# Rows of v before the small tables, state outputs on the Pool queue, and turned probabilities in four PSUM banks

## The chip, the cores and the metric

The kernel runs on one core of a Trainium2 chip. The core has TensorE (PE; PEld is its weight load), VectorE (DVE), ScalarE (ACT), GpSimd (POOL) and the synchronisation engine SyncE (SP). Transfers are issued from SP, ScalarE and Pool and carried out by 16 DMA engines that all three share. The metric is the device time of one launch in microseconds (us); lower is better. All data are float32.

## The reference

One inference step of a hybrid decoder layer, for a prompt of 2048 tokens and for 8 sample sequences of 4 new tokens each, which have 8192 past tokens in a paged cache:

```python
h = rmsnorm(x, norm_g)
z = jnp.einsum('btd,de->bte', h, w_in)
q_a, k_att, v_a, f_a, g_a, sh_b, g_b, u_c, g_c, u_d, g_d = split_cols(z)
logf = jax.nn.log_sigmoid((f_a + fox_bf).astype(jnp.float32))
o_a = attend(qh, kh, vh, logf)          # A: attention with forget gates
o_b, wkv1, shift1 = rwkv7_mix(sh_b, ...)  # B: RWKV-7, a matrix state
o_c, pool1 = pool_mixer(u_c, ...)       # C: causal pooling
o_d, conv1 = conv_module(u_d, ...)      # D: convolution, width 31
mixed = jnp.concatenate([o_a * silu(g_a), o_b * silu(g_b), o_c * silu(g_c), o_d * silu(g_d)], axis=-1)
x = x + jnp.einsum('bte,ed->btd', mixed, w_out)
return x, kh, vh, logf, wkv1, shift1, pool1, conv1
```

Two pieces matter here. The recurrence of B, run for four steps on the samples:

```python
s_kk = jnp.einsum('bhvk,bhk->bhv', s, kk_t)
s = s * w_t[:, :, None, :] - s_kk[..., None] * (kk_t * a_t)[:, :, None, :] + v_t[..., None] * k_t[:, :, None, :]
o = jnp.einsum('bhvk,bhk->bhv', s, r_t)
```

And the attention of the samples over the cache, whose scores take the running sum of log-forget values, and whose result is `softmax(scores) @ v_all`. Keys, values, log-forget values and states of the new tokens are outputs too.

## The kernel before

Each engine runs a program of its own, written out by hand; semaphores tie them together, and the order of the calls in each engine's function is the order of its work. Nothing is scheduled by a planner. Most data live in one large tile, `big`, whose areas are reused from stage to stage. The stages, in order of time:

*Projection.* TensorE multiplies h by 25 column groups of w_in (`chunk`, matmuls at L795), ScalarE copies each result out of PSUM (L1379) and stores it to the DRAM tensor `zT`. Convolution, pooling and the inputs of B run beside it on VectorE.

*Sample steps (about 740 to 840 us).* In the last column groups TensorE puts `sample_step(0)` to `sample_step(4)` (matmuls L906 and L914), with `value_rows` (L881) between them. Step i needs the state after step i-1, which VectorE makes in four operations (L1858 to L1862) from `v_row[i]`, and VectorE first multiplies all four `v_row` tiles (L1851). A `v_row` is one row of v for each of 8 sequences, written by ScalarE to the DRAM tensor `zsD` and read back by SP at L495, repeated over 64 partitions for each of two halves. Before these multiplies VectorE computes the index tables `pidx` and `lidx` (L1832 to L1838), for which it waits until six small loads, the last of them `aux`, have landed:

```python
dve.wait_ge(rows_in, 16 * 6)
```

Pool waits for these indices and then issues 64 gathers of log-forget rows (L757, tile `scores_`), and later 64 gathers of cached values, four of which may be under way.

*Prompt attention (about 914 to 1260 us).* TensorE goes through 32 items (16 query blocks, 2 head pairs): `scores`, `turn` (L988), `values` (L1001). From item 6 on, `early_keys` adds a step of the samples' scores (L1014), for which SP must have loaded 16 pages of keys (`key_pages`, L547). SP's loop over the items issues the page loads for the next step, which wait for the step before (`sc_mm`), stores an item's output and loads a gate. At item 11 it issues seven outputs (L557 to L564). VectorE's `forget_sums` (L1959) scans the gathered log-forget values, first after item 3.

*B over the prompt (about 1260 to 1540 us)*, with the other 16 steps of keys between its matmuls.

*Turned probabilities (about 1540 to 1590 us).* ScalarE takes exponentials of `scores_` in 8 blocks of 1024 columns. TensorE turns each block with 8 transposes into two PSUM banks (`turn_probs`), and ScalarE copies the two banks back (`probs_turned`, L1613). Blocks 0 and 1 are turned between two groups of the sums that normalise B's output (L1314), the others after them. ScalarE runs squares, the copies of blocks 0 and 1, then logarithms and exponentials (L1410), then the other copies.

*Output.* `value_tile` (L1051) multiplies turned probabilities by gathered values, 10 tiles first and 54 between the matmuls of the output projection (L1341).

Of the kernel before, what the change touches and what calls it, by code (L numbers as in the profile page):

```python
# [11 lines left out]
P = 128  # L12
D_MODEL, SEQ, DEC_BATCH, DEC_SEQ = 1024, 2048, 8, 4
SMP = DEC_BATCH * DEC_SEQ
T_ALL = SEQ + SMP
# [71 lines left out]
def build(nc, I, O):  # L87
    ctx = ExitStack()
    with ctx:
# [370 lines left out]
        def _(sp):  # L460
# [25 lines left out]
            sp.wait_ge(rw_stored, 128)  # L486
            sp.dma_start(wvf, I['w_vf']).then_inc(pars_in, 16)
# [4 lines left out]
            sp.wait_ge(v_spread, 16 * DEC_SEQ)  # L492
            sp.dma_start(s_wkv[0], I['state_T']).then_inc(s_in, 16)
            for i in range(DEC_SEQ):
                sp.dma_start(v_row[i], zsD[i].unsqueeze(1).to_broadcast([2, 64, 1024])).then_inc(x_in[i], 16)  # L495
# [53 lines left out]
            for j in range(len(ITEMS) - 2):  # L549
# [5 lines left out]
                if j == 11:  # L555
                    for t in range(2):
                        sp.dma_start(O['kT'][t], zT[KA + t]).then_inc(st_stored, 16)  # L557
                    sp.wait_ge(vf_evac, TT + 1)
                    sp.dma_start(O['v_prompt'][0, 0].rearrange("(n p) h d -> p n (h d)", p=P), vtok[:, 0:TT, 0:256]).then_inc(st_stored, 16)
                    sp.dma_start(O['v_sample'].rearrange("b l t h d -> (b l t) (h d)"), vtok[0:SMP, TT, 0:256]).then_inc(st_stored, 16)  # L560
                    sp.wait_ge(nl_ready, 2)
                    sp.dma_start(O['logf_prompt'][0, 0].rearrange("(n p) h -> p n h", p=P), lo[:, 0:TT, :]).then_inc(st_stored, 16)
                    sp.dma_start(O['logf_sample'].rearrange("b l t h -> (b l t) h"), lo[0:SMP, TT, :]).then_inc(st_stored, 16)
                    sp.dma_start(O['shiftE'], zT[R0:R0 + 7, :, SEQ - 1:T_ALL]).then_inc(st_stored, 16)  # L564
# [90 lines left out]
        def _(pool):  # L655
# [98 lines left out]
            pool.wait_ge(idx_ready, 1)  # L754

# [5 lines left out]
            for t in range(N_PAGES):  # L761
                x = 1 + (N_PAGES - 1 - t) * PAGE
                gather(scores_[:, x:x + PAGE], cf, lidx[:, t:t + 1], lf_in)
            pool.wait_ge(sc_mm, KSTEPS)
# [7 lines left out]
        def _(pe):  # L772
# [494 lines left out]
            def turn_probs(blk):  # L1267
                pe.wait_ge(D['p'], D0['p'] + blk + 1)
                if blk == 0:
                    pe.wait_ge(D['neg'], D0['neg'] + 1)  # L1270
                else:
                    pe.wait_ge(D['pT'], D0['pT'] + 2 * blk)
                rows = scores_[:, blk * 1024:(blk + 1) * 1024].rearrange("p (x j) -> p j x", j=TJ)
                for j in range(TJ):
                    last = transpose(psum[:, 6 + j // 4, (j % 4) * P:(j % 4 + 1) * P], rows[:, TJ - 1 - j, :])
# [1007 lines left out]
```

## Time and profile before

| | us |
|---|---|
| median of three timed runs | 1932.46 |
| lowest and highest | 1923.53 and 1933.47 |
| profiled execution, its own time | 1928.07 |
| its span, first to last instruction | 1926.3 |

| engine | busy us | share of the span |
|---|---|---|
| PE | 1773.4 | 92% |
| PEld | 1094.4 | 57% |
| DVE | 776.4 | 40% |
| ACT | 477.7 | 25% |
| POOL | 174.9 | 9% |

The profile is that of one execution. A busy time says how long an engine had instructions under way, and tells nothing of which engine the others wait for. For that one reads the chain of waits and the timeline of each engine: a timeline row gives start, duration, engine, line, what is written and read, the count of merged instructions and, in brackets, how long the engine had been idle and what ended that. Positions below are us from the start of the span. The names of SP's, ScalarE's and Pool's queues end in q.

### The profile page before, as it was taken

The numbers are of one execution on the slowest core, as the hardware profiler recorded it, in microseconds if no ns is written. First come the engines' busy times: TensorE is split into PE (matmuls) and PEld (weight loads), VectorE is DVE, ScalarE is ACT, GpSimd is POOL, SyncE is SP. The second block draws the span as 40 slices with busy tenths as digits, with TensorE's granted clock in tenths as the row PEclk, the third lists the DMA queues.
The fourth block names the chain that finished last, engine by engine and source line by source line (L and its number), as shares of the span: only waits on it lengthen the run. The fifth ranks groups of instructions, "written<-read, shape, count | busy, mean of one in ns | idle before, by whom it ended". The sixth has DMA issues, their size and how long they took to land.

```text
span 1926.3 us, 35542 instructions
## 1 busy us (share of the span) xinstructions
PE 1773.4 (92%) x15076; PEld 1094.4 (57%) x15076; DVE 776.4 (40%) x1640; ACT 477.7 (25%) x855; POOL 174.9 (9%) x220
## 2 busy tenths in 40 slices
PE   6999999999999999299697999998989878999997
PEld 3555555555554555286464677788878743444442
DVE  3450699742221541311553554435545551112112
ACT  4301100010327231002343454422222270000000
POOL 1000000011000003720000000000000002111210
PEclk9999999999999999699798999999999978999998
DMA  6223320376312345231565324467655267788782
GB/s 228 78 84 106 121 88 34 135 191 164 118 67 89 132 166 190 85 122 27 169 197 134 98 86 141 145 208 227 187 153 155 91 260 290 275 298 272 273 290 72
DMA packets 154512, 300.77 MB, mean 156 GB/s; under 512 B 20285, under 2 KB 124589, under 8 KB 136238
## 3 DMA queue, kind: packets, MB, share of 16 engines
q1 hardware_dynamic: 131746, 154.72, 25.8%
q0 software_dynamic: 18240, 115.82, 17.6%
q10 hardware_dynamic: 4368, 27.96, 3.6%
q8 instruction: 119, 1.95, 0.4%
q14 instruction: 39, 0.32, 0.0%
HBM read 236.73 MB, written 63.96 MB: 156 GB/s over the span
## 4 chain that ended last, share of the span: by engine, by line
PE 71%; DVE 13%; DMA 6%; ACT 4%; issue 3%; SPq 2%; another core or an unknown queue 1%; POOL 0%; ACTq 0%; DVEq 0%
PE psum L795 22%; PE psum L1051 13%; PE psum L1341 13%; DVE big L1733 8%; PE psum L988 6%; PE psum L1014 3%; PE psum L881 3%; PE psum L1001 3%; PE psum L975 2%; DMA big<-zsD 2%; ACT big L1410 2%; PE psum L775 2%; PE psum L827 1%; DMA rkv<-big 1%; DMA big<-zT 1%
## 5 line engine op out<-in xcount | busy, mean ns | idle before, releaser
L795 PE MATMUL psum<-big,wbuf 128*128 128x416 f32 x1920 | 675.8, 513 | 5.6 <-DVE big L1663 3.4
L795 PEld LDWEIGHTS psum<-big,wbuf 128*128 128x128 f32 x1920 | 364.9, 190 | 311.9 <-issue 310.2
L1051 PE MATMUL psum<-big 64*64 64x64 f32 (+3 forms) x5792 | 218.6, 263 | 25.3 <-issue 12.1
L1051 PEld LDWEIGHTS psum<-big 64*64 64x64 f32 (+2 forms) x5792 | 165.1, 132 | 87.8 <-issue 53.7
L1379 ACT ACTIVATE zst<-psum 128x416 f32<-128x416 f32 x125 | 64.0, 517 | 539.1 <-PE psum L795 539.0
L1341 PE MATMUL psum<-big 128*128 128x512 f32 (+1 forms) x408 | 186.5, 607 | 1.1 <-issue 1.1
L757 POOL DMA_INDIRECT big<-in_cache_v,pidx x64 | 60.6, 947 | 986.5 <-PE psum L1014 684.6
L1733 DVE SCALAR_TENSOR_TENSOR big<-big,pars 128x2048 f32<-128x2048 f32 x120 | 148.2, 1298 | 1.1
L1341 PEld LDWEIGHTS psum<-big 128*128 128x128 f32 (+1 forms) x408 | 73.5, 187 | 97.6 <-issue 97.6
L2175 DVE TENSOR_TENSOR zst<-zst,psum 128x1024 f32<-128x1024 f32 (+1 forms) x17 | 20.7, 1220 | 229.6 <-PE psum L1341 229.6
L1641 ACT ACTIVATE big<-zst 128x1024 f32<-128x1024 f32 (+1 forms) x17 | 18.0, 1057 | 301.1 <-DVE zst L2175 301.1
L988 PE MATMUL psum<-big,zst 128*128 128x128 f32 x544 | 72.8, 286 | 10.8 <-DVE big L1937 10.4
L1529 ACT COPY wbuf<-psum 128x512 f32<-128x512 f32 (+3 forms) x80 | 41.5, 519 | 165.5 <-PE psum L988 165.5
L975 PE MATMUL psum<-big 64*128 64x512 f32 (+3 forms) x320 | 74.3, 574 | 5.9 <-DVE big L1911 5.2
L988 PE MATMUL psum<-big 128*128 128x128 f32 x544 | 73.1, 287 | 5.9 <-DVE big L1937 5.4
L1001 PE MATMUL psum<-wbuf,big 128*64 128x128 f32 x544 | 77.8, 283 | 0.0
L1001 PE MATMUL psum<-big 128*64 128x128 f32 x544 | 77.8, 283 | 0.0
L988 PEld LDWEIGHTS psum<-big,zst 128*128 128x128 f32 x544 | 65.2, 194 | 20.3 <-DVE big L1937 11.4
L988 PEld LDWEIGHTS psum<-big 128*128 128x128 f32 x544 | 65.5, 195 | 15.4 <-DVE big L1937 7.6
L1001 PEld LDWEIGHTS psum<-wbuf,big 128*64 128x64 f32 x544 | 58.1, 138 | 26.7 <-issue 18.6
L1014 PE MATMUL psum<-big,lora 128*32 128x256 f32 x864 | 55.6, 399 | 18.7 <-DMA big<-in_k_pages 14.7
L757 POOL DMA_INDIRECT big<-in_logf_rows,lidx x64 | 65.3, 1020 | 34.9 <-issue 19.2
(240 smaller groups left out, 1839.4 us busy)
## 6 DMA issues: line engine op xcount, KB each, us to landing
big<-in_k_pages SPq DMA_DIRECT2D x432, 128.0 KB, 2.3
zT<-zst ACTq DMA_DIRECT2D x25, 1040.0 KB, 6.7
wbuf<-in_w_slots SPq DMA_DIRECT2D x24, 512.0 KB, 4.7
big<-zT POOLq DMA_DIRECT2D x11, 1024.0 KB, 5.6
zst<-in_k_pages SPq DMA_DIRECT2D x80, 128.0 KB, 2.5
rwS<-big POOLq DMA_DIRECT2D x8, 1024.0 KB, 4.2
big<-rwS SPq DMA_DIRECT2D x8, 1024.0 KB, 5.8
zst<-in_x_prompt SPq DMA_DIRECT2D x16, 512.0 KB, 8.5
```

The source lines that it names most:

```text
L757: g.indirect_dma_start(out=dst, out_offset=None, in_=cache, in_offset=bass.IndirectOffsetOnAxis(ap=idx, axis=0)).then_inc(s, 16)
L795: last = nc.tensor.matmul(psum[:, m % CHUNKS, 0:CW], w[:, k, :], hT[:, k, c * CW:(c + 1) * CW], start=(k == 0), stop=(k == KT - 1))
L881: last = nc.tensor.matmul(psum[0:r, n % CHUNKS, 0:VF], hT[:, k, n * P:n * P + r], wvf[:, k, :], start=(k == 0), stop=(k == KT - 1))
L975: last = nc.tensor.matmul(psum[:, 2 * (b % 2) + h, 0:w], kq[hs, 1, pr, i * P:(i + 1) * P], kq[hs, 0, pr, c * 512:c * 512 + w], start=True, ...
L988: last = nc.tensor.matmul(psum[:, 4 + h, k * P:(k + 1) * P], rows_[j % 2][h][:, x:x + P], diag[:, j % 2, h, :], start=True, stop=True)
L1001: last = nc.tensor.matmul(psum[h * 64:h * 64 + 64, 6 + j % 2, 0:P], vtok[:, k, (2 * pr + h) * 64:(2 * pr + h + 1) * 64], probsT[h][:, k * ...
L1014: last = nc.tensor.matmul(psum[32 * ct:32 * ct + 32, bank, 0:256].rearrange("p (i c) -> p i c", i=2), qbd[:, pr, b * 32:(b + 1) * 32], pag ...
L1051: return nc.tensor.matmul(out, l, r, start=start, stop=stop, skip_group_check=True)
L1341: last = nc.tensor.matmul(psum[0:n, 2 * u + o, :], l, wo[e][:, o * 512:(o + 1) * 512], start=(k == 0), stop=(k == 7))
L1379: nc.scalar.activation(zst[:, u, c * CW:(c + 1) * CW], psum[:, m % CHUNKS, 0:CW], f, scale=0.125 if n in (QA, QA + 1) else 1.0).then_inc(z ...
L1529: nc.scalar.copy(probsT[h][:, c * 512:c * 512 + width(j, c)], psum[:, 4 + h, 0:width(j, c)]).then_inc(pT_ready, 1)
L1733: last = v.scalar_tensor_tensor(out, in_, w, out, ALU.mult, ALU.add)
```

## The change

Four edits, all in the order of transfers, in waits and in bank numbers; the computation is the same.

1. SP issues the loads of `s_wkv[0]` and of the four `v_row` tiles before those of `wvf`, the masks, `bf_b` and `aux`.
2. Pool waits for the four `v_row` loads before its first gather.
3. The seven outputs of item 11 move from SP's loop to Pool, behind the log-forget gathers and a wait for 12 finished items.
4. `turn_probs` and `probs_turned` use banks 6 and 7 for even blocks and 4 and 5 for odd ones, and a turn waits for the copies of the block two before it.

```diff
             sp.wait_ge(rw_stored, 128)
+            sp.wait_ge(v_spread, 16 * DEC_SEQ)
+            sp.dma_start(s_wkv[0], I['state_T']).then_inc(s_in, 16)
+            for i in range(DEC_SEQ):
+                sp.dma_start(v_row[i], zsD[i].unsqueeze(1).to_broadcast([2, 64, 1024])).then_inc(x_in[i], 16)
             sp.dma_start(wvf, I['w_vf']).then_inc(pars_in, 16)
             sp.dma_start(dmask, I['diag_mask']).then_inc(rows_in, 16)
             sp.dma_start(rw_masks, I['rw_masks']).then_inc(rows_in, 16)
             sp.dma_start(bf_b, I['fox_bf'].to_broadcast([P, 4])).then_inc(rows_in, 16)
             sp.dma_start(aux[:, :], I['aux']).then_inc(rows_in, 16)
-            sp.wait_ge(v_spread, 16 * DEC_SEQ)
-            sp.dma_start(s_wkv[0], I['state_T']).then_inc(s_in, 16)
-            for i in range(DEC_SEQ):
-                sp.dma_start(v_row[i], zsD[i].unsqueeze(1).to_broadcast([2, 64, 1024])).then_inc(x_in[i], 16)
...
                 gate_store(j)
-                if j == 11:
-                    for t in range(2):
-                        sp.dma_start(O['kT'][t], zT[KA + t]).then_inc(st_stored, 16)
...
             pool.wait_ge(idx_ready, 1)
+            for i in range(DEC_SEQ):
+                pool.wait_ge(x_in[i], X_SEEN[i] + 16)
...
                 gather(scores_[:, x:x + PAGE], cf, lidx[:, t:t + 1], lf_in)
+            pool.wait_ge(o_read, 12)
+            for t in range(2):
+                pool.dma_start(O['kT'][t], zT[KA + t]).then_inc(st_stored, 16)
+            pool.wait_ge(vf_evac, TT + 1)
...
             pool.wait_ge(sc_mm, KSTEPS)
...
-                else:
-                    pe.wait_ge(D['pT'], D0['pT'] + 2 * blk)
+                elif blk >= 2:
+                    pe.wait_ge(D['pT'], D0['pT'] + 2 * (blk - 1))
...
-                    last = transpose(psum[:, 6 + j // 4, (j % 4) * P:(j % 4 + 1) * P], rows[:, TJ - 1 - j, :])
+                    last = transpose(psum[:, 6 - 2 * (blk % 2) + j // 4, (j % 4) * P:(j % 4 + 1) * P], rows[:, TJ - 1 - j, :])
...
-                    nc.scalar.copy(scores_[:, x:x + 512], psum[:, 6 + hf, :]).then_inc(D['pT'], 1)
+                    nc.scalar.copy(scores_[:, x:x + 512], psum[:, 6 - 2 * (blk % 2) + hf, :]).then_inc(D['pT'], 1)
```

SP's order of issue behind the last column weights, before (-) and with the change (+); `zsD x4` are the four rows of v:

```order
 L467 DMA wbuf<-in_w_slots 128x1024 x18
-L487 DMA big<-in_w_vf 128x2080
-L488 DMA big<-in_diag_mask 128x128
-L489 DMA big<-in_rw_masks 128x256
-L490 DMA big<-in_fox_bf 128x4
-L491 DMA big<-in_aux 128x128
-L493 DMA big<-in_state_T 128x1024
-L495 DMA big<-zsD 128x1x1024 x4
+L488 DMA big<-in_state_T 128x1024
+L490 DMA big<-zsD 128x1x1024 x4
+L491 DMA big<-in_w_vf 128x2080
+L492 DMA big<-in_diag_mask 128x128
+L493 DMA big<-in_rw_masks 128x256
+L494 DMA big<-in_fox_bf 128x4
+L495 DMA big<-in_aux 128x128
 L499 DMA qT_s<-zT 128x32
```

The rows of v moved ahead of five other loads, of which `aux` is the last.

Pool's order of issue behind the last stores of B's inputs, with the change (lines of the changed kernel; in_logf_rows are the log-forget gathers, in_cache_v those of values):

```order
83 L749 DMA big<-in_logf_rows,lidx 128x128 [waits x_in1,x_in2,x_in0,x_in3,idx_ready,rw_stored]
84 L749 DMA big<-in_logf_rows,lidx 128x128 x63
85 L758 DMA out_kT<-zT 32x8320 [waits o_read]
86 L758 DMA out_kT<-zT 32x8320
87 L760 DMA out_v_prompt<-big 128x16x256 [waits vf_evac]
88 L761 DMA out_v_sample<-big 32x256
89 L763 DMA out_logf_prompt<-big 128x16x4 [waits nl_ready]
90 L764 DMA out_logf_sample<-big 32x4
91 L765 DMA out_shiftE<-zT 896x33
92 L749 DMA big<-in_cache_v,pidx 128x2048 [waits sc_mm]
```

Before, Pool's gathers of values followed its log-forget gathers directly, and these waited for `idx_ready` and `rw_stored` alone; the seven outputs stood on SP between an item's gate load and the next page loads:

```order
187 L511 DMA pars<-zT 128x128 [waits mixa_stored0]
188 L557 DMA out_kT<-zT 32x8320 x2
189 L559 DMA out_v_prompt<-big 128x16x256 [waits vf_evac]
190 L560 DMA out_v_sample<-big 32x256
191 L562 DMA out_logf_prompt<-big 128x16x4 [waits nl_ready]
192 L563 DMA out_logf_sample<-big 32x4
193 L564 DMA out_shiftE<-zT 896x33
194 L542 TENSOR_LOAD pwo [waits sc_mm]
196 L547 DMA big<-in_k_pages 128x256
```

With the change L542 follows L511 directly. On TensorE no instruction moved; only the waits of `turn_probs` and its banks differ.

## Rows read from the trace of the kernel before

**Rows 1.** The page, part 4: the chain that ended last, by engine.

```profile
PE 71%; DVE 13%; DMA 6%; ACT 4%; issue 3%; SPq 2%; another core or an unknown queue 1%; POOL 0%; ACTq 0%; DVEq 0%
```

**Rows 2.** TensorE's timeline: start, duration (us), engine, line, what, count, idle before.

```profile
805.75 3.57 PE L906 MATMUL psum<-big,smp 64*64 64x64 f32 x64 [38.50 <-DVE big L1862]
```

**Rows 3.** VectorE's timeline, 748 to 941.

```profile
748.28 0.19 DVE L1832 CAST pidf<-pidx 128x64 f32<-128x64 int32 x1 [18.83 <-DMA big<-in_aux]
...
749.29 0.20 DVE L1838 CAST pidx<-pidf 128x64 int32<-128x64 f32 x1
...
760.84 1.23 DVE L1851 TENSOR_TENSOR big<-big,smp 128x1024 f32<-128x1024 f32 x1 [11.35 <-DMA big<-zsD]
...
799.55 1.23 DVE L1851 TENSOR_TENSOR big<-big,smp 128x1024 f32<-128x1024 f32 x1 [10.81 <-DMA big<-zsD]
800.70 1.22 DVE L1858 TENSOR_TENSOR big<-big,smp 128x1024 f32<-128x1024 f32 x1
...
940.39 2.29 DVE L1959 TENSOR_TENSOR_SCAN big<-big 128x1024 f32<-128x1024 f32 x1
```

**Rows 4.** DMA queues, 749 to 752: packets, MB, share of 16 engines.

```profile
q1 hardware_dynamic: 38, 0.16, 12.8%
```

**Rows 5.** DMA queues, 749 to 799: q0 is Pool's, q1 SP's.

```profile
q0 software_dynamic: 1148, 2.35, 14.7%
q1 hardware_dynamic: 1052, 2.13, 11.3%
```

**Rows 6.** SP's timeline.

```profile
770.99 13.07 SPq L499 DMA_DIRECT2D qT_s<-zT  x1
```

**Rows 7.** The loads of qT_s, from the issue's end to landing.

```profile
DMA to landing us min/median/max: 4.2/9.9/15.5
```

**Rows 8.** SP's timeline, 999 to 1017.

```profile
999.21 1.23 SPq L557 DMA_DIRECT2D out_kT<-zT  x2
...
1001.11 7.43 SPq L560 DMA_DIRECT2D out_v_sample<-big  x1
...
1016.57 8.93 SPq L547 DMA_DIRECT2D big<-in_k_pages  x16
```

**Rows 9.** TensorE's timeline, 998 to 1033.

```profile
998.45 1.93 PE L1014 MATMUL psum<-big,lora 128*32 128x256 f32 x32 [0.73 <-issue]
...
1029.67 3.64 PE L1014 MATMUL psum<-big,lora 128*32 128x256 f32 x32 [14.32 <-DMA big<-in_k_pages]
```

**Rows 10.** Stretches: length, busy PE, PEld, DVE, ACT, POOL; granted clock, DMA share, GB/s.

```profile
999.00:1016.00 17.00, 16.35 (x160) 12.09 (x151) 8.88 (x42) 9.80 (x19) 0.00 (x0) 1.00 0.87 262
...
1020.00:1030.00 10.00, 0.33 (x4) 0.20 (x8) 0.00 (x0) 0.00 (x0) 0.00 (x0) 0.50 0.87 232
...
1572.00:1590.00 18.00, 10.56 (x51) 8.46 (x50) 17.50 (x33) 6.54 (x13) 0.00 (x0) 0.64 0.27 96
```

**Rows 11.** Line L1613 (copies of turned blocks), who waited for it: us, times.

```profile
  PE psum L775: 11.8, 7
```

**Rows 12.** TensorE's timeline, 1555 to 1596.

```profile
1555.85 1.35 PE L775 MATMUL psum<-ident,big 128*128 128x128 f32 x8 [4.34 <-ACT big L1613]
...
1572.46 1.05 PE L775 MATMUL psum<-ident,big 128*128 128x128 f32 x8
...
1583.55 1.94 PE L775 MATMUL psum<-ident,big 128*128 128x128 f32 x8 [1.25 <-ACT big L1613]
...
1590.60 5.38 PE L1051 MATMUL psum<-big 128*32 128x256 f32 x64
```

**Rows 13.** ScalarE's timeline, 1557 to 1590.

```profile
1557.23 1.07 ACT L1613 COPY big<-psum 128x512 f32<-128x512 f32 x2 [1.53 <-PE psum L775]
...
1588.72 1.07 ACT L1613 COPY big<-psum 128x512 f32<-128x512 f32 x2 [2.12 <-PE psum L775]
```

**Rows 14.** Pool's timeline: the first and the last of 64 gathers.

```profile
750.36 1.03 POOL L757 DMA_INDIRECT big<-in_logf_rows,lidx  x1 [15.73 <-DVE pidx L1838]
...
832.87 1.99 POOL L757 DMA_INDIRECT big<-in_logf_rows,lidx  x1 [0.30 <-issue]
```

More of the change, by code:

```diff
@@ L554, in _ @@
                 gate_store(j)
-                if j == 11:
-                    for t in range(2):
-                        sp.dma_start(O['kT'][t], zT[KA + t]).then_inc(st_stored, 16)
[L558 to L564, printed above, removed]
             sp.wait_ge(st_stored, 16 * 7)
@@ L763, in _ @@
                 gather(scores_[:, x:x + PAGE], cf, lidx[:, t:t + 1], lf_in)
+            pool.wait_ge(o_read, 12)
+            for t in range(2):
+                pool.dma_start(O['kT'][t], zT[KA + t]).then_inc(st_stored, 16)
+            pool.wait_ge(vf_evac, TT + 1)
+            pool.dma_start(O['v_prompt'][0, 0].rearrange("(n p) h d -> p n (h d)", p=P), vtok[:, 0:TT, 0:256]).then_inc(st_stored, 16)
+            pool.dma_start(O['v_sample'].rearrange("b l t h d -> (b l t) (h d)"), vtok[0:SMP, TT, 0:256]).then_inc(st_stored, 16)
+            pool.wait_ge(nl_ready, 2)
+            pool.dma_start(O['logf_prompt'][0, 0].rearrange("(n p) h -> p n h", p=P), lo[:, 0:TT, :]).then_inc(st_stored, 16)
+            pool.dma_start(O['logf_sample'].rearrange("b l t h -> (b l t) h"), lo[0:SMP, TT, :]).then_inc(st_stored, 16)
+            pool.dma_start(O['shiftE'], zT[R0:R0 + 7, :, SEQ - 1:T_ALL]).then_inc(st_stored, 16)
             pool.wait_ge(sc_mm, KSTEPS)
```

## The prediction

> **What bounds the kernel now.** I read the page's chain of waits first: TensorE carries 71% of it, so time is won only where TensorE stands idle [rows 1]. Then I looked on TensorE's timeline for idle stretches beside the edited lines. There are three, one for each part of the change.
>
> *Place A, the sample steps.* TensorE idles 38.50 us before the second recurrence step at 805.75 [rows 2]. VectorE explains it: it multiplies four rows of v, the first at 760.84 after its load, the last at 799.55, having waited 10.81 us for it, and the chain L1858 to L1862 starts at 800.70 [rows 3]. From there to TensorE's restart are 5.05 us. So the loads of v decide, one row every (799.55 - 760.84) / 3 = 12.9 us for 512 KB.
>
> Why so slow? In 749 to 752 they are the only traffic: 0.16 MB in 3 us, 52 GB/s, with 12.8% of 16 engines busy, which is 2.05 engines [rows 4]. Two engines are full and fourteen empty. With the gathers of log-forget rows beside them (14.7% of 16 engines) they hold 11.3% over 50 us [rows 5]. The small load of qT_s, whose issue ended at 770.99 + 13.07 = 784.06, landed up to 15.5 us later, at 799.56, the same moment as the last row [rows 6, 7]. A transfer that is spread over all engines therefore waits on the two busy ones for all rows issued ahead of it. That is the fact that part one turns on.
>
> *Place B, the state outputs.* SP issues seven output transfers from 999.21 on, and the issue at L560 alone holds it 7.43 us. Only then do the 16 loads of key pages go out, from 1016.57 [rows 8]. TensorE waits 14.32 us for them, from 1015.35 to 1029.67, and its first group then takes 3.64 us against 1.93 for the same 32 matmuls at 998.45 [rows 9]: the granted clock was 0.50 in 1020 to 1030 and 1.00 before [rows 10].
>
> *Place C, the turned probabilities.* ScalarE's copies (L1613) held TensorE up 7 times, 11.8 us in total [rows 11]. Block 1 waits 4.34 us, until 1555.85; the blocks from 1572.46 on go one at a time, each turn waiting 1.25 us for the copy of the one before and taking 1.94 us, and the value matmuls start at 1590.60 [rows 12]. ScalarE in turn waits for each turn [rows 13].
>
> **The change, part by part.**
>
> *A.* The four rows and state_T move ahead of w_vf, the two masks, fox_bf and aux. About 1.3 MB leave the queue ahead of them: 81 KB for each engine, at 26 GB/s per engine (half of 52) 3.1 us, and some 4.5 us with ScalarE's store of zT that shares the engines; I take 4.5. The rows themselves, alone on two engines, need 2.1 MB / 52 GB/s = 40.4 us, and 2.5 us more for the zT store that falls between them, 43 us instead of the 50.4 they took (799 minus a start at 748.5, one 12 us row before the first landing). So the last row lands 12 us earlier, near 787.5.
>
> But VectorE's order is not changed. It first waits for all six small tables (L1832), aux among them, before any multiply of v. Today aux is in at 748.28 [rows 3] and this wait is covered by the rows. Now aux sits behind all four rows on the two full engines, with w_vf and the masks between (again 1.3 MB, 3.1 us, and about 0.5 us to land): near 791. Behind it come the index arithmetic, 748.28 to 749.49 (1.2 us), four multiplies at 1.15 to 1.23 instead of one (4.9 us in all), and the 5.05 us chain: TensorE restarts near 802.2, not 805.75. **A gains 3.5 us.** Bounds: 0 if w_vf and the tables go out late, and 12 if aux does not queue behind the rows (787.5 + 1.2 + 5.05 = 793.8).
>
> The gathers get a wait for all four rows, but they need the indices that VectorE writes after aux, so they start near 792 in any case, 42 us later. Behind them on the Pool queue now stand the seven outputs. The 64 gathers are issued in 832.87 + 1.99 - 750.36 = 84.5 us [rows 14], so they end near 877; the first scan that needs them is at 940.39 [rows 3]. Cover of 60 us; the cost is nothing.
>
> *B.* The seven outputs go to Pool, which is idle there, and SP is free at 999.2. It must still wait for the key step before (it ends at 1000.4), so the page loads go out from about 1001.5 (1.2 us after, as now). The outputs start at the same time, since Pool waits for the same twelve finished items. What lies between is engine time: the outputs filled 0.87 of all engines for 17 us (14.8 us), the pages 0.87 of them for 10 us (8.7 us) [rows 10]. If pages wait for all outputs they land near 999.2 + 14.8 + 8.7 = 1022.7: gain 7. If they go first they land before TensorE asks at 1015.35: gain 14.3. With equal shares the pages need twice 8.7 us from 1001.5, 1018.9: TensorE waits 3.6 us, gain 10.7. I take equal shares, because the nearest rows with two queues on one engine, the rows of v beside the gathers, show both advancing [rows 5]. The matmuls at half clock give back 3.64 - 1.93 = 1.7 us more. **B gains 12.4 us**, bounds 7 and 16.
>
> Here two rules of the Trainium skill bear. The page DMA: Bandwidth & Descriptors (Queues, rings and completion order) says that an engine takes turns between queues packet by packet; kT's packets would be long and the pages' short, so by it the pages would lose most turns until kT is through, and B would fall towards its lower bound. The page SBUF — State Buffer (SBUF: two separate sides) says that transfers issued on Pool wait for their descriptors while VectorE runs certain copies; by it the outputs would trail, the pages would win, and B would come to its upper bound. Rows 5 decide between neither.
>
> *C.* Even blocks keep banks 6 and 7, odd ones get 4 and 5, so a turn waits for the copy two blocks back. Block 1 is turned at once at 1555.85 - 4.34 = 1551.5, and ScalarE's copy of it no longer waits 1.53 us [rows 13]. The logarithms behind it start 1.5 us earlier, and TensorE's group sums, which wait for the first of them, end near 1570.9, not 1572.46. From there ScalarE's copies set the pace: 1.1 us for the first turn, six blocks at 1.1 us (1.07 for two copies and the handover), and the 0.8 us that lie between the last copy (1588.72 + 1.07) and 1590.60: 1579.4. Gain 11.2, and the first value tile, done at half clock today, should be 0.5 us quicker. **C gains 11.7 us.** If the clock falls as it does today (0.64 in 1572 to 1590, [rows 10]), turns at 1.94 us pace it: 1570.9 + 1.1 + 6 x 1.94 + 0.8 = 1584.4, gain 6.2; the upper bound is 13. Banks 4 and 5 are free until the value tiles, and VectorE's gated output, ready at 1591, is wanted only after ten value tiles, so nothing takes the place of this wait. Behind it, the value gathers hang on the tiles and move along.
>
> **Sum.** 3.5 + 12.4 + 11.7 = 27.6 us. Against the profiled execution's 1928.07 us this gives 1900.5; its span is 1926.3, the rest lies around it. That execution is 4.4 us under the median of the three timed runs, 1932.46, and inside their spread of 10 us. I say 1900.
>
> **The rivals.**
>
> 1. *The moved transfers only queue elsewhere* (18 us saved, 1910). A gives nothing because aux is late, and pages wait for kT and v_prompt (7 + 1.7, capped at 8). C pays 10, with the clock down for its last blocks. For it: rows 7 and 10. Against: A's tables follow the rows by only some 3 us.
> 2. *Aux does not wait* (A 12 instead of 3.5, B near 15, C 12; 39 saved, 1889). For it: the small tables are on sixteen engines and only two are full. Against: qT_s landed with the last row [rows 6, 7].
> 3. *The change does little* (within 9 us of before, 1925). The new banks would have to leave the copies in place as limit and the pages would have to land near 1028. For it: the pages' engine time is unchanged. Against: TensorE and ScalarE wait for each other in turn at C, which a second pair of banks breaks.
> 4. *Slower* (1935). The gathers start 42 us later and VectorE's scan of them at 940.39 sits in the middle of the attention loop; what it stalls, TensorE waits for. They take 1.25 us each. The scan is asked for at 937 now, so with 27.6 us of gains to eat up they must end after 965, which is 2.7 us each from 792 on; at 2.8 us each the time would be 1935. The longest single issue in the trace is 1.99 us [rows 14].
>
> **How the numbers follow.** The forecast (24 to 33 us saved, 1895 to 1904) has 0.56, rival 1 0.18, rival 2 0.14, rival 3 0.07, rival 4 0.03; 0.02 is left for anything else, mostly a small loss. The range reaches from rival 2 to rival 1: 1888 to 1911. A difference under 0.5% (9.7 us) is about what a measurement of this kernel cannot tell from none. Faster by more than that: 0.56 + 0.18 + 0.14 and a quarter of rival 3, 0.90; within it: 0.06; slower: 0.04.
>
> **What would show it.** A: rows of v every 10 us; VectorE's casts (L1832) no longer at 748 but after the last row; the idle before TensorE's second step only about 3 us shorter. If the casts come before the last row, rival 2 holds. B: page loads issued from about 1001.5 and a wait of 0 to 7 us before TensorE's fifth key step. C: turns in pairs without the 1.25 us waits, and value matmuls about 12 us after the casts' gain and B's are taken off. Wrong would be a wait for in_logf_rows before the scan L1959, or pages landing after the outputs.

## The result and the profile after

| | before | with the change |
|---|---|---|
| median of 10 runs each, us | 1923.78 | 1912.89 |
| lowest and highest, us | 1914.10 and 1933.47 | 1909.51 and 1919.03 |
| profiled execution, its own time, us | 1928.07 | 1909.78 |
| its span, us | 1926.3 | 1907.9 |

The ratio after to before is 0.9942, with a 95% interval of 0.9923 to 0.9961: the change makes the kernel 11.2 us faster (7.5 to 14.8). The forecast was 1900 with a range of 1888 to 1911, so the time lies just outside. The change brings 11.2 us, not 27.6, which is 16.4 us short. The base hid a part of that, by luck: I made the sum against 1928.07 us, and ten runs of the kernel before have their median at 1923.78, 4.3 us lower, so that the time missed the forecast by only 12.9 us.

The two profiled executions are 18.4 us apart, more than the medians. Part of that is not the change's: the last weights are issued at 735.38 instead of 737.13, and the B stage, in which nothing was edited, takes 507.75 us (from the fifth key step at 1023.99 to the group sums at 1531.74) against 510.82 before. So I compare lengths of idle stretches and distances between two fixed points of the program, not positions.

**Place A.** TensorE's timeline of the changed kernel behind its idle stretch (start, duration, engine, line, what, count, idle before):

```profile
802.86 3.68 PE L908 MATMUL psum<-big,smp 64*64 64x64 f32 x64 [37.37 <-DVE big L1864]
806.33 3.52 PE L916 MATMUL psum<-smp,big 64*64 64x1 f32 x64
809.78 9.53 PE L883 MATMUL psum<-big 128*128 128x260 f32 x32
```

The same piece of the kernel before, behind the row in [rows 2]:

```profile
809.16 1.98 PE L914 MATMUL psum<-smp,big 64*64 64x1 f32 x64
811.07 7.31 PE L881 MATMUL psum<-big 128*128 128x260 f32 x32
```

The idle stretch shrank from 38.50 to 37.37 us, by 1.1. But the three groups behind it take 3.68 + 3.52 + 9.53 = 16.7 us instead of 3.57 + 1.98 + 7.31 = 12.9: the clock came back later. Read for one microsecond at a time, the granted clock of the kernel before is 0.50 until 809 and 0.96 in 809 to 810, so full speed returns 3.4 us after the restart; in the changed kernel it is 0.50 until 814 and 0.84 in 814 to 815, so it returns after 11.5 us. The rows over the whole piece say the same:

```profile
803.00:843.00 40.00, 40.00 (x536) 35.50 (x538) 14.62 (x12) 2.33 (x6) 30.55 (x32) 0.86 0.16 53
```

```profile
806.00:842.00 36.00, 36.00 (x534) 32.16 (x532) 14.44 (x12) 2.33 (x6) 22.47 (x22) 0.96 0.14 44
```

(First the changed kernel, then the one before; columns as in [rows 10].) Net, place A loses 2.7 us. VectorE's timeline, changed kernel, shows what the stretch ends on:

```profile
792.13 0.20 DVE L1834 CAST pidf<-pidx 128x64 f32<-128x64 int32 x1 [64.43 <-DMA big<-in_aux]
...
793.27 1.22 DVE L1853 TENSOR_TENSOR big<-big,smp 128x1024 f32<-128x1024 f32 x1
794.40 3.49 DVE L1853 TENSOR_TENSOR big<-big,smp 128x1024 f32<-128x1024 f32 x3
797.81 1.22 DVE L1860 TENSOR_TENSOR big<-big,smp 128x1024 f32<-128x1024 f32 x1
```

The first cast waits for `aux` until 792.13, where before it ran at 748.28 [rows 3]; the multiplies of all four rows then run in one go, so all rows were there. SP was held up too: its issues of the four rows took 24.4 us and that of `w_vf` 12.4 (0.43 before), so that `aux` was issued only from 776.20 on, and it landed 15.9 us later. The queue still moved 52 GB/s with 12.8% of the engines in 788 to 790, so rows were under way until then. The rows had the DMA engines to themselves, and still used 2.05 of 16 (12.8%), as in [rows 4]; queues of the changed kernel, 745 to 757:

```profile
q1 hardware_dynamic: 153, 0.62, 12.8%
```

The last log-forget gather starts at 876.26, and the scan (L1961 there) runs at 939.83 with no wait ahead of it, so rival 4 did not come in.

**Place B.** The timelines of Pool, SP and TensorE, changed kernel:

```profile
998.90 1.24 POOL L760 DMA_DIRECT2D out_v_prompt<-big  x1
```

```profile
1000.74 15.20 SPq L547 DMA_DIRECT2D big<-in_k_pages  x16
```

```profile
1023.99 3.64 PE L1016 MATMUL psum<-big,lora 128*32 128x256 f32 x32 [9.47 <-DMA big<-in_k_pages]
```

The pages are issued 15.8 us earlier than in [rows 8], but their issue now takes 15.20 us instead of 8.93, and from its start to the matmuls pass 23.25 us instead of 13.10. Of the 15.8 us most is gone. The queues show where, in three stretches, 1000 to 1005, 1007 to 1012 and 1013 to 1018 (packets, MB, share of 16 engines; q0 is Pool's, q1 SP's; shares can sum to over 100% since packets of two queues overlap):

```profile
q0 software_dynamic: 66, 1.66, 97.7%
q1 hardware_dynamic: 14, 0.01, 0.4%
...
q0 software_dynamic: 399, 1.63, 80.9%
q1 hardware_dynamic: 400, 0.36, 21.2%
...
q1 hardware_dynamic: 471, 0.43, 92.9%
q0 software_dynamic: 137, 0.20, 25.6%
```

In the first stretch kT runs, in packets of 33 KB (50 of the 80 packets are over 8 KB and carry all of the 1.66 MB), and the pages get nothing: from 1001 to 1005 Pool's queue moved 60 packets and SP's none, in 1005 to 1006 SP's moved 3 and in 1006 to 1007 68. From then on, while v_prompt runs, both queues get the same number of packets, 399 and 400, but Pool's carry 4.1 KB and SP's 0.9 KB, so the pages get 18% of the bytes. Then come the log-forget outputs, whose rows are 16 bytes long; bandwidth falls to 126 GB/s.

**Place C.** TensorE's timeline, changed kernel:

```profile
1538.79 1.95 PE L777 MATMUL psum<-ident,big 128*128 128x128 f32 x16
1542.20 3.03 PE L1316 MATMUL psum<-big,ones_head 128*128 128x416 f32 x8 [1.45 <-ACT big L1412]
1549.89 6.98 PE L1316 MATMUL psum<-big,ones_head 128*128 128x416 f32 x12 [4.66 <-ACT big L1412]
1556.71 7.15 PE L1316 MATMUL psum<-zst,ones_head 128*128 128x416 f32 x20
1563.69 1.94 PE L777 MATMUL psum<-ident,big 128*128 128x128 f32 x16
1565.98 2.10 PE L777 MATMUL psum<-ident,big 128*128 128x128 f32 x16 [0.36 <-ACT big L1615]
1568.37 2.11 PE L777 MATMUL psum<-ident,big 128*128 128x128 f32 x16 [0.29 <-ACT big L1615]
```

Blocks 0 and 1 are turned together (16 transposes in 1.95 us), the others in pairs, with waits of 0.3 us instead of 1.25. The copies held TensorE up for 1.8 us in 3 waits, where [rows 11] had 11.8 in 7:

```profile
  PE psum L777: 1.8, 3
```

The value matmuls start 40.54 us after the first group sum (1531.74 to 1572.28); before it was 50.11 (1540.49 to 1590.60, [rows 12]): 9.6 us won.

### The profile page after: what moved, and what is told of

Read it like the earlier page. It is cut to its first block, busy times and chain, and to the rows that moved or that the text cites. A ratio compares the mean times of both kernels' runs of the same rounds, so it can differ in the third digit from the quotient of the medians.

```text
span 1907.9 us, 35544 instructions
## 1 busy us (share of the span) xinstructions
PE 1765.4 (93%) x15076; PEld 1090.5 (57%) x15076; DVE 776.5 (41%) x1640; ACT 477.5 (25%) x855; POOL 178.8 (9%) x227
## 3 DMA queue, kind: packets, MB, share of 16 engines
q8 instruction: 119, 1.95, 0.4%
## 4 chain that ended last, share of the span: by engine, by line
PE 71%; DVE 13%; DMA 5%; ACT 4%; SPq 3%; issue 3%; POOL 0%; ACTq 0%; DVEq 0%
PE psum L797 22%; PE psum L1053 13%; PE psum L1343 13%; DVE big L1735 8%; PE psum L990 6%; PE psum L883 3%; PE psum L1016 3%; PE psum L1003 3%; PE psum L977 3%; ACT big L1412 2%; PE psum L829 1%; SPq L490 1%; DMA rkv<-big 1%; PE psum L777 1%; SPq L547 1%
## 5 line engine op out<-in xcount | busy, mean ns | idle before, releaser
L749 POOL DMA_INDIRECT big<-in_logf_rows,lidx x64 | 63.8, 997 | 80.5 <-DVE pidx L1840 61.3
```

The lines of the kernel that those rows point to most:

```text
L749: g.indirect_dma_start(out=dst, out_offset=None, in_=cache, in_offset=bass.IndirectOffsetOnAxis(ap=idx, axis=0)).then_inc(s, 16)
```

## The experiments

Each was timed in five rounds beside the kernel before. Ratios are to the kernel before, with their 95% intervals.

| | edit | median us | ratio |
|---|---|---|---|
| e1 | part A alone | 1927.36 | 1.0011 (0.9993 to 1.0028) |
| e2 | part B alone | 1923.01 | 0.9994 (0.9975 to 1.0013) |
| e3 | part C alone | 1915.58 | 0.9957 (0.9939 to 0.9974) |
| e4 | before, rows of v in halves | 1884.50 | 0.9800 (0.9776 to 0.9824) |
| e5 | before, outputs early | 1912.14 | 0.9919 (0.9888 to 0.9949) |
| e6 | before, gathers held and `wvf` behind the rows | 1916.98 | 0.9957 (0.9937 to 0.9977) |
| e7 | before, gathers held | 1918.68 | 0.9964 (0.9946 to 0.9983) |
| e8 | e4, e5 and part C | 1860.33 | 0.9654 (0.9625 to 0.9683) |
| e9 | change, tables ahead | 1909.36 | 0.9914 (0.9892 to 0.9937) |
| e10 | change, kT early | 1909.43 | 0.9924 (0.9900 to 0.9948) |
| e11 | change, log-forget outputs early | 1912.94 | 0.9930 (0.9907 to 0.9953) |

### e1, e2, e3: the parts alone

e1 has the SP order and Pool's waits for the rows alone, e2 the seven outputs on Pool alone, e3 the four banks alone, each as in the diff above.

> Only edits 1 and 2 on the kernel before: rows of v before w_vf and the tables, gathers behind the rows. Theory (the profile after: aux lands at 792, four multiplies follow it, the gathers run on into the value rows): no gain, -2 to +2 us, ratio 0.999 to 1.001. Rival (my first sum): 3.5 us faster, ratio 0.998. In both the casts at L1832 start near 790, not 748.

> Only edit 3 on the kernel before: the seven outputs on Pool. Theory (the key pages wait for kT's long packets and then take turns with 4096-byte packets while theirs have 1024 bytes): TensorE's wait before the fifth key step is still about 9.5 us of 14.3; 5 us faster, ratio 0.9974. Rival (equal shares, my first sum): a wait near 4 us and 12 us faster, ratio 0.994.

> Only edit 4 on the kernel before: odd blocks in banks 4 and 5. Theory: the value matmuls start 9 to 10 us earlier, ratio 0.995. Rival (my first sum): 11.7 us, ratio 0.994. Rival 2: the profile's gain there is chance and the ratio is above 0.998.

By these ratios A costs 0.1%, B brings 0.1%, C brings 0.4%; A and B can't be told from nothing. e1 and e3 came out near their first theories. e2 did not: 0.9974 was expected, just below its interval, and TensorE's wait is 10.31 us, not 9.5. The sum of the three is 0.38%, just under the interval of the whole change (0.39% to 0.77%); with the intervals of the three it is compatible with it, and nothing shows that the parts need each other. Two of three brought nothing that can be told. e1's profile repeats place A of the changed kernel, with the same late return of the clock:

```profile
802.29 3.68 PE L908 MATMUL psum<-big,smp 64*64 64x64 f32 x64 [37.43 <-DVE big L1864]
805.75 3.53 PE L916 MATMUL psum<-smp,big 64*64 64x1 f32 x64
```

For B, the distance between the starts of the fourth and the fifth key step is 31.2 us before (998.45 to 1029.67, [rows 9]), 29.2 in e1 (997.02 to 1026.26) and 28.9 in e3 (998.10 to 1027.04), which have the outputs where they were, as have e6 and e7 below with 29.2 and 29.6. With them on Pool it is 26.4 in the changed kernel (997.62 to 1023.99), 27.2 in e2 (997.15 to 1024.36) and 27.7 in e9. By the means, 29.6 and 27.1, B wins 2.5 us here. For C, from the first group sum to the output projection pass 73.6 us before (1540.49 to 1614.08) and 72.9 to 74.1 in the six others with two banks (e1, e2, e4, e5, e6, e7); with four banks 64.5 in the changed kernel (1531.74 to 1596.21), 62.0 in e3 (1539.70 to 1601.72) and 63.8 to 65.0 in e8 to e11. C wins 9.6 by the means, 73.4 and 63.9.

### e4: the rows of v on sixteen engines

```diff
-                sp.dma_start(v_row[i], zsD[i].unsqueeze(1).to_broadcast([2, 64, 1024])).then_inc(x_in[i], 16)
+                for h in range(2):
+                    sp.dma_start(v_row[i][h * 64:(h + 1) * 64, :], zsD[i, h].unsqueeze(0).to_broadcast([64, 1024])).then_inc(x_in[i], 16)
```

The waits on `x_in` count both transfers. Nothing else differs from the kernel before.

> The kernel before with each row of v loaded in two transfers, one for each half of the partitions, so that the outer size of each is 64 and not 2; order and everything else as before. Theory (a transfer with outer size 2 runs on 2 of 16 engines, and nothing else makes the rows slow): all four rows land within 10 us, before 765; TensorE's idle of 38 us before the second sample step goes, 35 to 40 us faster, ratio 0.981. Rival (the rows are slow because they all read one 4 KB stretch of DRAM, or because of the gathers): the rows still take 10 us each and the time stays within 0.3%.

It took 1884.50 us, 2.0% less, more than three times what the change brings. Queues of e4, 749 to 752, and VectorE's first and last multiply of a row:

```profile
q1 hardware_dynamic: 219, 0.72, 104.6%
```

```profile
751.28 1.23 DVE L1852 TENSOR_TENSOR big<-big,smp 128x1024 f32<-128x1024 f32 x1 [3.26 <-DMA big<-zsD]
...
758.11 1.23 DVE L1852 TENSOR_TENSOR big<-big,smp 128x1024 f32<-128x1024 f32 x1 [1.21 <-DMA big<-zsD]
```

In the same stretch as [rows 4] 0.72 MB move instead of 0.16, on all sixteen engines; a row comes every 2.3 us instead of 12.9, and TensorE's 38.5 us of idling are gone. The slowness of the rows was the shape of one transfer, whose outer size is 2. The Trainium skill says so, DMA: Bandwidth & Descriptors (Why a DMA increments its semaphore by 16 and not by 1, and Rules for kernel authors): the size of the slowest dimension decides how many engines a transfer gets, and one of c < 16 confines it to at most c. The traces agree: 2.05 engines at outer size 2, all sixteen at 64. All of part A is a change of order around a transfer that should have had another shape.

### e5: the outputs early

The kernel before with the outputs on Pool directly behind the 64 log-forget gathers, with no wait for an item (`z_ready` waits for the stores of k):

```diff
                 gather(scores_[:, x:x + PAGE], cf, lidx[:, t:t + 1], lf_in)
+            z_ready(KA)
+            z_ready(KA + 1)
+            for t in range(2):
+                pool.dma_start(O['kT'][t], zT[KA + t]).then_inc(st_stored, 16)
+            pool.wait_ge(vf_evac, TT + 1)
...
```

> The kernel before with one edit: the seven outputs go through Pool, but directly behind the 64 log-forget gathers (they wait only for the stores of k, not for twelve items), so they start near 830 to 845 us, when the DMA engines are little used, and not near 1000. Theory 1 (in the change the outputs and the pages of keys still meet on the engines, the engines take turns between the queues packet by packet, and pages of 1 KB packets get a fifth of the bytes while outputs of 4 to 33 KB packets run; that is why moving them to Pool brought little): with the outputs gone from 1000 us, SP issues the pages of the fifth key step at about 1001.5 and they land near 1011 to 1013, before TensorE asks at 1015, so TensorE waits 0 to 1 us there and its first matmul group takes 1.9 us instead of 3.6. Saved 14 to 16 us against the profile before, 8 to 14 by the medians (the wait has varied between executions); ratio 0.993 to 0.996. Theory 2 (TensorE's wait before the fifth key step is not what ends the kernel's critical path, or is given back later): the wait goes, the time does not move, ratio 0.998 to 1.001. Theory 3 (outputs laid elsewhere delay something else, such as the first pages of keys near 880 to 940): a new wait of 5 us or more ahead of the fourth key step.

The ratio is 0.9919, 13 to 16 us, a little more than expected. Pool, SP and TensorE in e5:

```profile
830.57 1.13 POOL L757 DMA_DIRECT2D out_kT<-zT  x2
```

```profile
999.29 9.44 SPq L547 DMA_DIRECT2D big<-in_k_pages  x16
```

```profile
1013.00 1.93 PE L1015 MATMUL psum<-big,lora 128*32 128x256 f32 x32
```

The fifth key step has no wait and runs at full clock (1.93 us instead of 3.64). The distance from the fourth to the fifth is 16.8 us instead of some 29.6. The wait was therefore on the path and worth about its full length. e2 changed the queue alone, and e5 the queue and the time. What part B lacked was the time: on Pool or on SP, the outputs met the pages on the same engines.

### e10 and e11: which output holds the pages up

In the changed kernel, e10 issues only the two kT outputs early and e11 only the two log-forget outputs:

```diff
+            z_ready(KA)
+            z_ready(KA + 1)
+            for t in range(2):
+                pool.dma_start(O['kT'][t], zT[KA + t]).then_inc(st_stored, 16)
             pool.wait_ge(o_read, 12)
-            for t in range(2):
-                pool.dma_start(O['kT'][t], zT[KA + t]).then_inc(st_stored, 16)
```

> The changed kernel with one edit: of the seven outputs the two of kT (packets of 33 KB) go on the Pool queue directly behind the log-forget gathers; the other five stay behind the wait for twelve items. Theory 1 (engines take turns packet by packet, so pages of 1 KB packets get next to nothing beside kT and a fifth beside v_prompt's 4 KB packets): pages move from the start; v_prompt's 2.1 MB need about 10 us with 0.5 MB of pages beside them, the rest of the pages and the tiny packets of logf follow; TensorE's wait before the fifth key step falls from 9.5 to about 3 us (2 to 5), 5 to 7 us under the changed kernel, ratio to before 0.990 to 0.992. Theory 2 (the tiny packets of the log-forget outputs hold the engines, kT costs little): the wait stays at 7 to 9 us, the time within 2 us of the changed kernel.

> The changed kernel with one edit: of the seven outputs only the two of the log-forget values (33 KB in packets of 16 bytes) go out early; kT, v_prompt, v_sample and shiftE stay. Theory 1 (packets, not bytes, take an engine's turn): the stretch of 1013 to 1018, in which 0.63 MB moved at 126 GB/s, goes at 250 GB/s or more, the pages land near 1019 to 1021 instead of 1023.5 and TensorE's wait falls from 9.5 to 5 to 7 us; 2 to 4 us under the changed kernel. Theory 2 (33 KB are nothing, bytes decide): wait 9 to 10 us, time unchanged within 1 us.

TensorE's fifth key step in e10, then in e11:

```profile
1019.26 3.64 PE L1018 MATMUL psum<-big,lora 128*32 128x256 f32 x32 [5.61 <-DMA big<-in_k_pages]
```

```profile
1023.87 3.64 PE L1016 MATMUL psum<-big,lora 128*32 128x256 f32 x32 [6.43 <-DMA big<-in_k_pages]
```

From the issue of the pages to these matmuls pass 17.4 us in e10 (from 1001.86) and 20.2 in e11 (from 1003.68), against 23.25 in the changed kernel. But in e10 SP issued the pages 5.1 us after the fourth key step had started, in the others 3.1. By the distance between the two key steps, 22.5 us in e10 and 23.3 in e11 against 26.4, kT costs 3.9 us and 33 KB of log-forget values cost 3.1.

The log-forget values are small but hold the engines. Alone, early in e11 (892 to 894), they are 78 packets with 0.03 MB and fill 60.6% of all engines for 2 us. In e11 the stretch 1015 to 1020 moves 254 GB/s, where the changed kernel had 126 in 1013 to 1018; in e10, which keeps them beside the pages, 1005 to 1014 moves 117 GB/s. So bytes do not decide. The number of packets does not either: 608 moved in the slow stretch of the changed kernel and 1138 in that of e11. What was long is each packet, 0.16 us for one of SP's against 0.07 (92.9% of 16 engines for 5 us over 471 packets, 88.6% over 988). The reason was not tried.

One part of e10's first theory failed: the pages did not move from the start. Issued from 1001.86 on, beside v_prompt alone, they had no packet before 1005, while v_prompt moved 308 packets from 1001 to 1005. With the engines free, in e5, the first 166 packets moved in 1000 to 1001, issued from 999.29. So the delay before SP's first packet is not kT's alone, and equal turns describe only what comes behind it. What causes it stays open.

In time the two experiments are not certain: e10 is 3.5 us under the changed kernel, e11 level with it, and both intervals overlap that of the change. e10's wait of 5.6 us lies above the 2 to 5 that I expected.

### e6, e7 and e9: what the rows of v wait for

e7 is the kernel before with Pool's waits for the rows alone. e6 also moves `wvf` behind the rows, but leaves the four small tables ahead. e9 is the changed kernel with the four tables ahead:

```diff
+            sp.dma_start(dmask, I['diag_mask']).then_inc(rows_in, 16)
+            sp.dma_start(rw_masks, I['rw_masks']).then_inc(rows_in, 16)
+            sp.dma_start(bf_b, I['fox_bf'].to_broadcast([P, 4])).then_inc(rows_in, 16)
+            sp.dma_start(aux[:, :], I['aux']).then_inc(rows_in, 16)
             sp.wait_ge(v_spread, 16 * DEC_SEQ)
             sp.dma_start(s_wkv[0], I['state_T']).then_inc(s_in, 16)
...
             sp.dma_start(wvf, I['w_vf']).then_inc(pars_in, 16)
```

> The kernel before with two edits: only w_vf is moved behind the state and the rows of v (masks, fox_bf and aux stay ahead of them), and Pool waits for the four rows before its gathers. So the rows are loaded with nothing of Pool's beside them, as in the change, but the index tables are not late. Theory 1 (the change's first part gave nothing because VectorE's first multiplies wait for aux, which queues on the two full engines behind the rows): VectorE's casts are near 748, the last row lands near 787 to 790, TensorE's second recurrence step starts near 793 to 796 instead of 805.8. Saved 9 to 12 us at the restart, less 1 to 3 us if the matmuls behind it again run at a lower clock as in the change; ratio 0.994 to 0.996. Theory 2 (the rows are paced by their two engines whatever is beside them, so freeing these from the gathers gives nothing): the last row lands near 798 as before and the ratio is 0.999 to 1.001.

> The kernel before with one edit: Pool waits for the four rows of v before its gathers; the order of SP's loads is that of before. It isolates the gathers' share of the two busy engines. By the rows of before the four rows take 50.4 us with the gathers beside them and 2.1 MB / 52 GB/s = 40 us plus the stores of z alone. Theory 1: last row 7 to 8 us earlier, near 791 to 792, TensorE restart near 797 to 799; ratio 0.995 to 0.997. Theory 2 (gathers take nothing from the rows): last row at 799, ratio 0.999 to 1.001.

> The changed kernel with one edit: masks, fox_bf and aux are loaded ahead of the state and the rows of v again (only w_vf stays behind them). It undoes the one thing that theory 1 blames for the first part's lack of effect: VectorE's multiplies waiting for aux behind the rows. Theory 1: TensorE's second recurrence step starts near 796 instead of 802.9, and the time falls by 5 to 8 us under that of the changed kernel (1912.9), to 1905 to 1908; ratio to the kernel before 0.990 to 0.992. Theory 2 (the gain shown with this order in the kernel before does not carry over, since the fifth key step or the clock takes it back): 1911 to 1914, ratio 0.993 to 0.995.

TensorE behind its idle stretch in e7, then in e9:

```profile
797.43 3.68 PE L908 MATMUL psum<-big,smp 64*64 64x64 f32 x64 [31.49 <-DVE big L1864]
800.90 2.36 PE L916 MATMUL psum<-smp,big 64*64 64x1 f32 x64
803.19 7.31 PE L883 MATMUL psum<-big 128*128 128x260 f32 x32
```

```profile
795.58 3.68 PE L908 MATMUL psum<-big,smp 64*64 64x64 f32 x64 [29.85 <-DVE big L1864]
799.05 3.52 PE L916 MATMUL psum<-smp,big 64*64 64x1 f32 x64
802.50 9.84 PE L883 MATMUL psum<-big 128*128 128x260 f32 x32
```

| | idle before, us | three groups behind, us | sum |
|---|---|---|---|
| before | 38.50 | 12.9 | 51.4 |
| changed kernel | 37.37 | 16.7 | 54.1 |
| e7, gathers held | 31.49 | 13.4 | 44.8 |
| e6, and `wvf` behind | 30.01 | 17.1 | 47.1 |
| e9, change with tables ahead | 29.85 | 17.0 | 46.9 |

e6 and e7 came out as their first theories said: VectorE takes the last row at 789.96 and 791.16, and both ratios lie in the range expected. The one order that differs between e9 and the changed kernel is that of four small tables, and it is worth 7.5 us of idling. Holding the gathers alone (e7) shortens the idling by 7.0 us, and the time by 6.9. Moving `wvf` as well (e6) shortens the idling by another 1.5 us and loses 3.8 to the clock. e6 saved 8.3 us in time and only 4.3 in this table; how late the clock returns over all its runs is not known. e9 is 3.5 us under the changed kernel by the medians and 5.4 by the ratios, around the lower end of what I expected, with intervals that overlap.

The clock's late return is no accident of one execution. In the six profiles with `w_vf` behind the rows (changed kernel, e1, e6, e9, e10, e11) the granted clock stays at 0.50 until 11.2 to 12.2 us after TensorE's restart, and the third group takes 9.50 to 9.93 us. In the five with `w_vf` ahead of them (before, e2, e3, e5, e7) it returns after 3.3 to 4.3 us, and the third group takes 7.31. The idle stretch is no longer in the first kind (29.9 to 37.5 us against 31.5 to 38.6), and TensorE's instructions are the same. What in that order does it was not tried.

### e8: what the experiments point to

Rows of v in halves, outputs behind the gathers, four banks.

> The rows of v in halves of 64 partitions (which took 0.980 of the time before), the outputs on Pool directly behind the gathers, and the turned probabilities in four banks. Theory 1 (each idle stretch of TensorE stands on the critical path by itself and the gains add): 1884.5 for the halves, less 8 to 14 for the outputs, less 8 for the banks: 1862 to 1869, ratio 0.967 to 0.971. Theory 2 (a stretch won early is waited for later, as at item 11 or in the RWKV stage): 1870 to 1880, ratio 0.972 to 0.977.

1860.33 us, 3.5% under before; the three ratios multiplied (0.9800, 0.9919, 0.9957) give 0.968, inside the interval of e8 (0.9625 to 0.9683), so the gains add. The time is even a little under the 1862 to 1869 expected. TensorE runs through the sample steps with no idle stretch:

```profile
758.90 5.85 PE L797 MATMUL psum<-big,wbuf 128*128 128x416 f32 x16
764.68 2.08 PE L908 MATMUL psum<-big,smp 64*64 64x64 f32 x64
766.60 1.98 PE L916 MATMUL psum<-smp,big 64*64 64x1 f32 x64
```

## Why the prediction was wrong, point by point

**A, forecast 3.5 us, found none (-2.7 in the profile; e1 0.1% slower).** The mechanism was right: `aux` landed behind the rows on two full engines and VectorE waited for it, at 792.13 where the text had 791. The last row's time was about right too: in e9, where nothing hides it, VectorE takes it at 789.30, and the text had 787.5. Two terms were off. The idle stretch fell by 1.1 us and not 3.5: the last weights went out 1.75 us earlier in this execution, so that `aux` was late by 2.9 us against my sum. And the sum took the groups behind the restart at the durations of before, 3.57, 1.98 and 7.31; they took 3.8 us more, because the clock stayed at half for longer. I had no term for that: the sum put the clock's return at nothing. It came 3.4 us after the restart in the kernel before and 11.5 in the changed kernel, and late in every profile with `w_vf` behind the rows; why stays open.

The evidence for the mechanism was misread. The times to landing in [rows 7] count from the start of an issue, not from its end: `aux`, issued at 739.78 and landed 8.5 us later, is the 748.28 of [rows 3]. So the first load of qT_s landed by its row at 786.5, not at 799.56 with the last row. The four loads of qT_s and kT_s share one semaphore, so that only the last of them can be read with certainty: issued at 786.88, it landed 13.6 us later, at 800.5, right behind the last row. The conclusion held, the row named for it did not show it.

**The gathers** cost nothing where I looked, at the scan. That they took engine time from the rows was in the forecast (43 instead of 50.4 us), and e7 shows it alone: 7.0 us. In the change the wait for `aux` hid it.

**B, forecast 12.4 us, found 2.5 in the profiles (1.2 by e2's time, -2.5 to 4.8).** Here a step failed, and not only a size: "With equal shares the pages need twice 8.7 us". TensorE waited 9.47 us for the pages, not 3.6. I took equal shares from rows of v beside gathers, but [rows 5] does not show them. Its sums are over all engines: the rows filled 11.3% of sixteen, 1.8 engines' worth on two engines, and the gathers 14.7%, which spread evenly is some 0.3 on these two (an estimate). On the shared engines the rows thus had six parts in seven, and the gathers did not press: Pool issued one about every 1.3 us (84.5 us for 64 [rows 14]). Here both queues were full. SP's had no packet for some 4 us after its first issue, and then equal turns with very unequal packets, 399 against 400 packets but 1.63 against 0.36 MB.

The rule on turns packet by packet, named in the prediction from the Trainium skill, DMA: Bandwidth & Descriptors (Queues, rings and completion order), pointed the right way. The traces agree with it from 1006 on, and do not show it before, when SP's queue got no turn. B fell below even its lower bound of 7. That bound had the pages behind all outputs near 1022.7, 24.3 us after the fourth key step; the fifth started 26.4 us after it, so they came later still, which the prediction had named as a sign of being wrong. What the sum of engine time lacked is the slow stretch of 126 GB/s behind v_prompt. And the bound counted from the 1029.67 of one execution: the distance between the two key steps is 31.2 us there and 29.6 as a mean of five profiles with the outputs on SP. And the matmuls stayed at half clock, 3.64 us, so the 1.7 us for them did not come; in e5, without a wait, they did (1.93). The second rule I named there, that Pool's transfers wait while VectorE runs, did not show: the seven outputs were issued from 997.81 to 1003.10 without a gap. But VectorE ran no copy in that time, so this tests the rule little.

**C, forecast 11.7 us, found 9.6 in the profile, 9.6 over thirteen, 8.3 by e3's time (5.0 to 11.7).** Mechanism right, size a little high. The turns came in pairs and from the end of the group sums to the first value matmul passed 8.6 us (1563.69 to 1572.28), as computed (1570.9 to 1579.4, 8.5). The step "the group sums ... end near 1570.9, not 1572.46" did not hold in the profiled execution: from their start to the next turn it is 31.95 us (1531.74 to 1563.69), before 31.97. ScalarE's logarithms did start earlier, but TensorE had waited 4.66 us for them and did the next 12 matmuls in 6.98 us at a lower clock (0.62 granted in 1549 to 1557). In e3 it had waited 3.38 us, the clock there was 1.00, the same 12 took 4.46 us and the piece was 29.4 us long (1539.70 to 1569.13), better than forecast. So this term is one of the clock, different from one execution to the next.

**The base.** The three runs shown of before had their median at 1932.46, ten have it at 1923.78, later groups at 1925 to 1926. The profiled execution, on which the sum rests, lies 3 to 4 us above these. I took its place under the median of three runs for a sign that it was not high. From the right base the forecast would have been near 1896, so this error helped, by luck.

**The rivals.** Rival 1, with a chance of 0.18, named what happened: the moved transfers only queue elsewhere. It gave A nothing and B at most 8 us, and 1910; the time is 1912.9, since B brought less still.

## What to carry to other kernels

Before you reorder transfers around a slow one, multiply its share by 16: if that gives two engines and not sixteen, change the transfer's shape first (here 2.0% against 0.6% for the whole change). Where a bulk transfer and an urgent one meet, price the urgent one by packets: here it got no turn for some 4 us, and then one for each of the other's, of 4.1 KB against its 0.9; moving the bulk to another queue at the same time brought next to nothing (e2), moving it to a time at which the engines were idle did (e5). And a small load that an engine waits for first must not be behind a slow one (7.5 us of idling between e9 and the changed kernel), even if the slow one carries what everybody waits for.

## What the runs showed of the hardware beyond that

- One output has other packets on another queue: v_prompt went through SP in packets of about 1 KB (in 1008 to 1016, kernel before, 1968 packets of 512 B to 2 KB carry nearly all of 2.05 MB), through Pool in packets of 4.1 KB (399 for 1.63 MB). The log-forget outputs (2048 rows of 16 bytes and a few more) are most of the 2111 packets under 512 B on SP in the same stretch, and 78 packets on Pool in e11. If turns are equal, the move to Pool made the outputs stronger against the pages than packets of 1 KB would have been; no run shows that alone.
- SP's issue of 16 page loads is no fixed cost: from 995 to 1060 it took 8.1 to 9.9 us in all profiles where no output of Pool's ran beside it, and 13.7 to 15.3 us where Pool's outputs filled the engines.
- The clock's return after an idle stretch of 30 to 39 us took between 3.3 and 12.2 us of work, with the same instructions on TensorE. The eleven profiles with such a stretch fall into two groups, 3.3 to 4.3 and 11.2 to 12.2, by the place of one transfer, `w_vf`, in SP's order.
